# The plain one-hot operand of the gate matrix, made on ScalarE instead of VectorE

## The reference, cut to what matters

```python
def block(args):
    xc, ec, gc = args
    act = jax.nn.gelu(jnp.einsum('nd,nkd->nk', xc, u_tab[ec]).astype(jnp.float32), approximate=False)
    return jnp.einsum('nk,nkd->nd', gc * act, v_tab[ec])
```

## Time and profile before

| | |
|---|---|
| time, median of 3 runs | 4158.34 us (4156.69 to 4164.11) |
| time of the profiled execution | 4160.88 us |
| span of the profiled execution | 4158.7 us, mean granted TensorE clock 0.942 |
| busy: TensorE, weight load, VectorE, ScalarE, GpSimd | 90%, 76%, 60%, 7%, 17% of the span |
| HBM traffic | 302 GB/s over the span |
| stage of the one-hot sets | from about 2221 to 2431 us of the span |

### The profile page before, as it was taken

One profiled execution on the slowest core, in us unless ns is written; L12 is line 12 of the kernel. 1 busy time (PEld: TensorE's weight loads), 2 busy tenths in 40 slices (PEclk: granted clock), 3 DMA queues, 4 the chain that ended last, 5 costly groups with the idle time before them and its releaser, 6 DMA issues.

```text
span 4158.7 us, 50821 instructions
## 1 busy us (share of the span) xinstructions
PE 3741.5 (90%) x21387; PEld 3147.9 (76%) x21387; DVE 2510.9 (60%) x4071; ACT 289.7 (7%) x733; POOL 711.9 (17%) x629
## 2 busy tenths in 40 slices
PE   6899799999997899897995779999998998989897
PEld 4677677777786788786874668888787887878786
DVE  3319920003589975665777856666667666676765
ACT  1010110010000010000001200000000000000000
POOL 1000000000000022221222222222223222232330
PEclk7899899999998899998997989999999999999999
DMA  9565354574432279995776879999999999999995
GB/s 334 202 248 183 116 183 181 190 255 173 152 132 82 92 296 389 388 395 209 284 289 238 296 288 420 421 421 421 418 421 413 421 421 404 421 421 421 418 415 230
DMA packets 205018, 1258.35 MB, mean 303 GB/s; under 512 B 20039, under 2 KB 53311, under 8 KB 53990
## 3 DMA queue, kind: packets, MB, share of 16 engines
q1 hardware_dynamic: 84631, 611.24, 38.0%
q0 software_dynamic: 85648, 616.08, 36.5%
q10 hardware_dynamic: 34512, 27.79, 2.0%
HBM read 1226.75 MB, written 28.64 MB: 302 GB/s over the span
## 4 chain that ended last, share of the span: by engine, by line
DMA 39%; PE 35%; DVE 20%; issue 4%; POOL 1%; ACT 0%; DVEq 0%; SPq 0%; ACTq 0%; POOLq 0%
PE banks L576 25%; DMA arena<-peer_v,arena 22%; DMA arena<-peer_u,arena 14%; PE banks L855 5%; DVE arena L1229 3%; DVE arena L1220 3%; PE banks L599 2%; PE banks L558 1%; POOL arena L504 1%; DMA arena<-w_ada 1%; DVE arena L1883 1%; PE banks L881 1%; DVE arena L1517 1%; DVE arena L1880 1%; DMA y_prompt<-arena 0%
## 5 line engine op out<-in xcount | busy, mean ns | idle before, releaser
L855 PE MATMUL banks<-arena 128*128 128x256 f32 x8192 | 1808.9, 384 | 103.5 <-DVE arena L1907 78.0
L855 PEld LDWEIGHTS banks<-arena 128*128 128x128 f32 x8192 | 1573.4, 193 | 332.2 <-issue 95.7
L576 PE MATMUL banks<-arena 128*128 128x288 f32 (+1 forms) x6464 | 1542.3, 400 | 30.8 <-DVEq L1201 19.5
L576 PEld LDWEIGHTS banks<-arena 128*128 128x128 f32 x6464 | 1239.7, 193 | 303.0 <-DVEq L1201 21.0
L1229 DVE SCALAR_TENSOR_TENSOR arena<-arena 128x2048 f32<-128x2048 f32 x285 | 670.1, 2351 | 378.2 <-DMA arena<-peer_v,arena 376.5
L1220 DVE SCALAR_TENSOR_TENSOR arena<-arena 128x2048 f32<-128x2048 f32 x288 | 657.2, 2293 | 336.9 <-DMA arena<-peer_u,arena 324.7
L504 POOL DMA_INDIRECT arena<-peer_u,arena x288 | 360.5, 1252 | 2053.4 <-DVE arena L1220 1420.1
L504 POOL DMA_INDIRECT arena<-peer_v,arena x288 | 325.1, 1129 | 802.0 <-DVE arena L1229 728.7
L558 PE MATMUL banks<-arena 128*128 128x128 f32 (+4 forms) x445 | 86.6, 340 | 82.7 <-DVEq L1871 33.7
L1111 ACT ACTIVATE arena<-banks 128x256 f32<-128x256 f32 x128 | 49.0, 383 | 1396.3 <-PE banks L855 1396.2
L558 PEld LDWEIGHTS banks<-arena 128*128 128x128 f32 (+4 forms) x445 | 58.2, 169 | 110.7 <-DVEq L1871 34.1
(11 more groups left out here) (254 smaller groups left out, 1604.6 us busy)
## 6 DMA issues: line engine op xcount, KB each, us to landing
arena<-peer_ut SPq DMA_DIRECT2D x128, 1024.0 KB, 9.2
arena<-peer_vd SPq DMA_DIRECT2D x128, 1024.0 KB, 9.2
arena<-w_ada SPq DMA_DIRECT2D x96, 1024.0 KB, 6.9
arena<-w_in SPq DMA_DIRECT2D x96, 1024.0 KB, 4.9
arena<-w_out SPq DMA_DIRECT2D x32, 1024.0 KB, 8.8
arena<-peer_wq SPq DMA_DIRECT2D x32, 1024.0 KB, 4.9
arena<-w_proj_b SPq DMA_DIRECT2D x16, 1024.0 KB, 4.9
arena<-w_proj_a SPq DMA_DIRECT2D x16, 1024.0 KB, 8.2
```

Of the source, the lines that this page charges most:

```text
L576: last = mm(out, w, src[:, b, :], start=k == 0, stop=k == len(blocks) - 1)
L855: last = mm(dense_out(m), slab16[j][:, k, :], rows[:, k, :], start=k == 0, stop=k == KD - 1)
```

## The change

VectorE no longer makes the plain operand. ScalarE makes it in a new function, `second_hot(q)`: for each of the four tokens |index - lane| (`Abs` with scale -1 and the index column as bias, 128 x 128), then for all four relu(1 - that) in place (`Relu` with scale -1 and a column of ones as bias, 128 x 512), which is one at the equal lane and zero elsewhere. Sets 0 and 1 are made before the loop, set q + 2 right after the copy of set q. TensorE waits for a second semaphore before each set. The columns are signalled to ScalarE as `columns_laid`, which replaces the two waits that VectorE had there.

```diff
             def one_hots(q):
 
                 pe.wait_ge(s["onehot_ready"], q + 1)
+                pe.wait_ge(s["second_hot_ready"], q + 1)
                 if q >= 4:
                     pe.wait_ge(s["g_read"], q - 3)
...
             act.wait_ge(s["gt2_saved"], 32)
+
+            def second_hot(q):
+
+                if q >= 2:
+                    act.wait_ge(s["g_made"], q - 1)
+                out = hot[q % 2][0]
+                for j in range(4):
+                    own.did(fn(out[:, j, :], lane, ACT.Abs, scale=-1.0, bias=slot_rows[:, 1, 4 * q + j:4 * q + j + 1]))
+                own.settle()
+                fn(out, out, ACT.Relu, scale=-1.0, bias=iota16[:, 1:2]).then_inc(s["second_hot_ready"], 1)
+
+            act.wait_ge(s["columns_laid"], 1)
+            second_hot(0)
+            second_hot(1)
             for b in range(16):
...
                        GATE[q % 4].rearrange("p (t c j) -> p t c j", t=4, c=16), ACT.Copy).then_inc(s["g_read"], 1)
+                    if q + 2 < TP // 4:
+                        second_hot(q + 2)
...
-            settle()
-            pf.settle()
+            signal("columns_laid")
             for q in range(TP // 4):
                 if q >= 2:
                     dve.wait_ge(s["g_made"], q - 1)
-                did(tt(hot[q % 2][0], bc(lane, 1, 4), bc(slot_rows[:, 1, 4 * q:4 * q + 4], 2, 128), ALU.is_equal))
                 for j in range(4):
```

More of the change, by code:

```diff
@@ L112 @@
 head_ready keys_laid expand_ready xn_ready dve_stood gt2_ready x1_saved gt2_saved late_ready late_exp slots_laid
-onehot_ready g_made g_read h_read gate_done sum_read dense_done buf_used act_ready gelu_ready acc_ready fin_in
+columns_laid onehot_ready second_hot_ready g_made g_read h_read gate_done sum_read dense_done buf_used act_ready gelu_ready acc_ready fin_in
 fin_sum fin_row fin_out rows_made fold_read""".split()
```

## The result

The changed kernel is slower: 4174.32 us in the median of 8 runs (4168.70 to 4176.45), against 4164.67 for 8 runs of the kernel before beside it; the ratio is 1.0029, 95% interval 1.0017 to 1.0040. The profiled execution took 4172.09 us with a span of 4169.0, against 4160.88 and 4158.7 before.

The account below looks back on a forecast made before the run. VectorE was late in the one-hot stage; with the change ScalarE paces runs. First group 22.34 plus the rest 183.65 gave 205.99 us against 208.79, 2.8 less: 4155.5 us, no change (chance 0.50), range 4144 to 4174.

Parts of the forecast that it names:

- a group of six sets with the change: One-hot stage, one dense to the next: dense, first copy, four ScalarE periods, last set; 18.67 us, 18.86 on average with stores.
- over the sum: The whole one-hot stage, added up from its groups: 205.99 us against 208.79 before, 2.8 us less.
- the first group: Start of the one-hot stage, with a first dense of 9.72 us: 22.34 us, against 24.92 before.
- TensorE's clock falls: Slower rival: 1.41 us of standing after each set lowers the clock; 10 us slower, 4168, or 4177; chance 0.14.
- VectorE's part: One-hot stage: a comparison of 0.69 us a set goes, 1.25 us a set is left, 153 us in all; VectorE has room.
- ScalarE's period: ScalarE's time for one set in a run, copy plus four `Abs` plus `Relu`: 2.38 us, which sets the pace.
- the bounds of 1.85 and 2.90: ScalarE's period in us: lower with a free bias column and closer `Abs`, upper with no overlap of instructions.
- both rivals that hung on them: Bias column free: some 13 us less, 4145, chance 0.26; ScalarE's instructions do not overlap: 19 us slower, 4177, chance 0.10.
- the dot products hidden at that pace: VectorE's pair, 4.6 us, mostly hides behind two sets made ahead and a dense; the stops of 5 us go.
- the end moving by what the stage moved: After the one-hot stage: gathers keep the DMA engines busy with the same bytes, so the program's end shifts by as much.
- The 0.37 us to issue a store: In every second group, one store issued on ScalarE inside the path; raises the group from 18.67 to 18.86 us on average.
- the prediction's second estimate of a period: ScalarE's period from the Trainium skill's activation costs and overlap: 2.41 us, making the sum 1.3 us higher.

Follow-up runs that it names:

- e1: Changed kernel with three extra matmuls (fillers, result thrown away) ahead of each of sets 3 to 6 of a group; stage 204.32 us, 0.9994 of before.
- e2: Kernel before with 19 extra matmuls ahead of each set that stands 5.3 us for VectorE's two dot products; stage 202.49 us, 0.9993 of before.
- e4: Changed kernel with the six sets of a group between the blocks of a dense product and the GELU one group later; stage 184.16 us, 0.9958 of before.
- e3: Changed kernel without the `Relu` and its wait, so the plain operand holds the distance; stage 193.68 us, 0.9971 of before.
- e7: Changed kernel with one extra matmul, not three, ahead of each of sets 3 to 6 of a group; stage 220.41 us, 1.0035 of before.
- e9: Kernel before with one VectorE dot product after every second set, not two after every fourth; stage 220.05 us, 1.0028 of before.

## Why the prediction was wrong

The forecast was no change, 4155.5 us; measured is slower by 0.29 per cent, and 4174.32 us lies just past the end of the range. Of the 16 us between 4158.34 and 4174.32, though, 6.3 are not the change's: the kernel before took 4164.67 us beside it. The change itself costs 9.65.

The step that failed is the sum for "a group of six sets with the change". It took 6.80 us for the dense and 0.89 for the last set from rows at the full clock. In the changed kernel ten dense products together take 7.3 us more than 6.78 each (0 at 2244.09, rising to 1.02 at 2426.05), and nine last sets 0.67 to 0.81 more than 0.97, another 7.0. That is 14.3 us, and the stage is 12.4 us over the sum. e1 puts the clock back and finds 204.3 us, 1.7 under the sum; the first group alone is 1.6 under it (20.77 us for 22.34), mostly since its dense took 8.71 us and not 9.72.

The mechanism stood among the rivals, "TensorE's clock falls", priced at 10 to 19 us, and was given 0.14. The time came out at the low end of that, by smaller losses: 7.3 us on the dense products and not 12.8, 7.0 on the last sets and not 9. The reason for so little was the row with pauses of 0.90 us at clock 1.00. It was weighed as if it spoke for 1.41 us too, which no row showed. The text also said that only the stops of 5 us show the clock low, and that these go: they went, and the clock stayed at 0.90 on average over the stage, as against 0.89 before. And the trace of the kernel before had a row against it, a set that slows after a pause of 0.90 and ahead of its long stop (the clock is 0.84 from 2390 to 2392 us):

```profile
2390.97 1.45 PEld L881 LDWEIGHTS banks<-arena 128*128 128x128 f32 x8 [0.90 <-DVEq L1886]
```

The rule of the Trainium skill that was set beside this rival ("TensorE: Matmul & The Clock Gate", "A second HAM failure mode: psum-queue depth-cycling") says that short, frequent standing between groups of matmuls lets the clock go to and fro. At 1.43 us the trace of the changed kernel agrees with it; at 0.90 us the trace does not, while e2 and the row above do.

What held: VectorE's part (1.25 us a set, room to spare); ScalarE's period, 2.40 for 2.38, with `Abs` 0.389 for 0.39, every 0.29, and `Relu` 0.72 for 0.71, so that the bounds of 1.85 and 2.90 and both rivals that hung on them fell; the dot products hidden at that pace but for the 0.8 us at a fifth set, which the sixth made up; the end moving by what the stage moved. Two small things were wrong. The 0.37 us to issue a store does not lie in the path, since it runs beside the `Relu` (both start at 2256.39). And the prediction's second estimate of a period, 2.41 us, adds up to 2.43 by the figures given with it (0.52 + 3 x 0.294 + 0.387 + 0.03 + 0.61). The balance itself, 1.87 us a set with stops against 2.38 without, comes out as forecast when fillers hold the clock in the changed kernel, and in part in the kernel before (e1 and e2): no gain.

## What to carry to other kernels

Moving work off a late engine to an idle one only swaps the name of the waiter if the idle one takes longer per step in the same chain; compare the period of the chain before and after, and not the busy times. If the new period leaves TensorE standing longer between its bursts, price the next burst at the lower clock, unless rows show the clock held at that very pause, in every group and not in one: at 0.90 us it was held in some groups here and lost in others. Then look for order: here the change paid only once other matmuls stood between the sets (e4), or once ScalarE's step was 1.65 us (e3), and of the change and the mixed order neither gained alone.

## What the runs showed of the hardware that was not expected

TensorE's clock in this kernel, by what it did in runs of paced sets of about 0.97 us:

- It was held at 1.00 in every full group with three fillers a set (e1), with pauses of 0.77 us, and of 1.29 and 1.51 among them.
- With pauses of 0.90 behind a first of about 1.2 it was held in the groups of four paced sets (before, e2), but lost at the fourth set in every second group of e2, and once in the kernel before.
- With a filler and pauses of 1.21 (e7) it was held through one group of ten, and with pauses of 1.43 (changed) through none.
- It was lost at single stops of 3.11 (e9), 3.74 (e3) and 5.32 us (before), or within two sets behind them.

So the length of a pause alone does not decide, and what else does stays open. Three extra matmuls a set whose result is thrown away (e1) made the stage 14 us shorter than without them. Where the fall lands matters as much as that it comes: behind it a dense took 6.8 to 7.8 us in the changed kernel, and 8.96 in e9.
